# A two-block transformer stage in float32: the rotated partner of each head's features is fetched by transfers between partitions

## Chip, cores and metric

One Trainium2 chip, one core of it. The metric is the device time of one launch in microseconds (us), as a median of several runs; lower is better. Inputs and outputs are float32, and the products are made from pairs of rounded parts (hi and lo), three products for each.

## The reference

Two blocks of two layers each run on 512 tokens of 1024 features. Only the first block's heads matter here. In each of its two layers the normed input is projected to queries, keys and values of three kinds of heads (differential, retention, grouped-query), and the queries and keys get a rotary embedding:

```python
def apply_rope(x, cos_sin):
    cos, sin = cos_sin
    n = x.shape[-1] // 2
    ...
    x1, x2 = x[..., :n], x[..., n:]
    return jnp.concatenate([x1 * c - x2 * s, x2 * c + x1 * s], axis=-1)
...
        dq = partial_rope(rms_norm(dq.reshape(B, S, DIFF_HEADS, 2, DIFF_HEAD_DIM), diff_q_norm[l]))
        rq = apply_rope(rq.reshape(B, S, RET_HEADS, RET_KEY_DIM), rope_ret).astype(f32)
        gq = axial_rope(rms_norm(gq.reshape(B, S, GQA_KV_HEADS, GQA_GROUP, GQA_HEAD_DIM), gqa_q_norm[l]))
```

Differential heads rotate the first 16 of 64 features (two heads' maps side by side: tables at features 0 and 64, half width 8). Retention heads rotate all 128 (half width 64). Grouped-query heads rotate in four groups of 32 (half width 16). Each rope is x times a cosine table plus the partner feature, with a sign, times a sine table.

## The kernel before, in words

**Layout.** Features lie on the 128 partitions and the 512 tokens along the free axis, so the partner of a feature lies on another partition. A weight chunk is 128 columns of a weight matrix over 1024 rows, 512 KB.

**A chunk.** SyncE (SP) loads a chunk into one of four slots of `wraw` (`RAW = 4`): `slot(chunk)` waits until chunk - 4 is done on TensorE (`chunk_done`), so each load goes out when a chunk ends. ScalarE rounds it to `whi` (`weight_hi`, L1702), VectorE makes `wlo` (`weight_lo`, L2300), and TensorE (PE) runs 24 matmuls over it (`chunk_product`, L1053 to L1055), in four parts of six.

**The order.** `head_schedule` writes each layer's heads as a list of steps with due times; the unit is one part, and a chunk is four (`PARTS`). All engines walk the same list in the order of the due times, each taking the steps that are its own, so a step that waits holds back everything behind it on its engine. A layer has 34 such chunks; 21 of them are queries or keys with a rope: 5 of grouped-query heads (chunks 0, 1, 3, 4, 5), 8 of differential heads (every third chunk is a value), 8 of retention heads (two of four). Below, rope 0 to rope 20 are these 21 of the first layer in their order; the second layer repeats them. Chunks 0 and 1 end almost together, the others follow four units apart.

**A rope** with a norm, counted from the end of its projection: ScalarE squares and copies the bank to `rawb` (L1897, L1899); PE sums the squares (`head_norm`, L1196, end + 1.5); ScalarE makes the inverse root (L1734, L1737, end + 1.9); VectorE scales `rawb` (`head_scale`, L2432, end + 2.4) and raises `qn_ready`; PE multiplies `rawb` with a signed permutation matrix from `mats` (`rotate`, L1206, end + 3.5) into one of two AUX banks of PSUM; VectorE makes t1 = x cos (L2441), t2 = partner sin (L2443), and adds them (L2452) (`roped`, end + 3.9), and raises `rope_done`. Without a norm (retention) rotate is due at end + 0.5 and roped at end + 0.9.

**Units.** Between the parts stand the attention units, 32 in a layer, one every 2.85 units of due time from 18 on (numbered unit 0 to unit 31 here). One unit is: two scores (PE, L1222), `peak` (VectorE, negated row maxima, L2468, 0.5 after), `softmax` (ScalarE, L1937, 0.9 after), `weigh` (VectorE, reciprocals and scaling, L2485 to L2495, 1.7 after), `turn` (PE, four transposes, L1234, 2.6 after), `turned` (ScalarE), and after four units `attend` (L1250, L1253). `lo` steps (L2300) stand 1.8 after a unit's start, just behind its weigh. Retention scores (L1228), their weighing by `decay` (L2478) and the final norms are placed between. After the heads come 24 gate chunks and 12 branch chunks, then the output product and the MLP.

**SP** walks the same list and issues only the weight chunks; a pair chunk (grouped-query) is two transfers (L955, L958), the second after the first has landed.

Of the kernel before, what the change touches and what calls it, by code (L numbers as in the profile page):

```python
# [11 lines left out]
ALU = mybir.AluOpType  # L12
AX = mybir.AxisListType

P = 128
# [46 lines left out]

class Step:
# [24 lines left out]
def head_schedule(layer, num):  # L88
# [126 lines left out]
def number_steps(order, num, last):  # L215

    for s in order:
# [19 lines left out]
        elif name == "rotate":  # L237
            s.rope.rot_aux, s.rope.rot = num["aux"](), num["rot"]()
        elif name == "roped":
            r = s.rope  # L240
            r.free_after = 0 if r.hd is None else last.get(("scored", r.hd - 2), 0)
# [253 lines left out]
class Plan:  # L495


    def __init__(self):
# [4 lines left out]
            "gqa mean split final gate norm norm_tile mlp_tile residual x_turn").split()}  # L503
# [45 lines left out]
def constants():  # L549
# [8 lines left out]
    def table(blocks):  # L558
        cos, sin = np.ones((P, SEQ)), np.zeros((P, SEQ))
        rot = np.zeros((P, P))  # L560
        for at, ang in blocks:
            n = ang.shape[1]
            for half in range(2):
                cos[at + half * n:at + (half + 1) * n] = np.cos(ang).T
                sin[at + half * n:at + (half + 1) * n] = np.sin(ang).T
            for j in range(n):
                rot[at + n + j, at + j] = -1.0
                rot[at + j, at + n + j] = 1.0
        return cos, sin, rot
# [9 lines left out]
    mats = np.stack([t[2] for t in tables] + [halves, np.ones((P, P))]).astype(f)  # L579
# [20 lines left out]
def build(nc, a, out):  # L600
    plan = Plan()
    ctx = ExitStack()
    with ctx:
# [25 lines left out]
        mats = sb("mats", [P, 5, P], scope=one_scope)  # L629
# [46 lines left out]
        decay = sb("decay", [P, TOEPLITZ], scope=head_scope)  # L676
        head_scope.close()
# [92 lines left out]
        rot_done, rope_done, turn_done, score_done = sem("rot_done"), sem("rope_done"), sem("turn_done"), sem("score_done")  # L770
# [74 lines left out]
        def _(sp):  # L845
# [102 lines left out]
            for s in plan.layers:  # L948
# [10 lines left out]

                for step in s.heads:  # L960
                    if step.name == "part" and step.index == 0:
                        whole = step.head
                        if whole.chunk == RAW:
                            tables()
                        if whole.kind == "pair":

                            w, at = a["w_in"][l].rearrange("(k p) c -> p k c", p=P), whole.columns
                            half_chunk(whole.chunk, lambda x: [
                                x.rearrange("p (k two c) -> p k two c", two=2, c=64)[:, :, i] for i in range(2)],
                                w[:, :, at:at + 64], w[:, :, at + 256:at + 320])  # L970
                        else:
                            column_chunk(whole.chunk, a["w_in"][l], whole.columns)
                    elif step.name == "branch":
                        w = a["w_branch"][l, step.n][:, 2 * P * step.pair:2 * P * (step.pair + 1)]
                        if step.n == 2:

                            w = w.rearrange("(g j p) c -> g p j c", g=2, p=64)
                            half_chunk(step.chunk, lambda x: [
                                x[64 * g:64 * (g + 1)].rearrange("p (k c) -> p k c", c=2 * P) for g in range(2)], w[0], w[1])
                        else:  # L980
                            r = slot(step.chunk)
                            sp.dma_start(wraw[:, r, :].rearrange("p (k c) -> p k c", c=2 * P),
                                         w.rearrange("(k p) c -> p k c", p=P)).then_inc(raw_in[r], 16)
                    elif step.name == "gate":
                        column_chunk(step.chunk, a["w_in"][l], GATES + D * step.n + P * step.d)
                for j in range(KT):
# [50 lines left out]
        def _(pe):  # L1037
# [47 lines left out]
            def first_sum(k):  # L1085
                pe.wait_ge(sq_ready, k + 1)
                pe.matmul(ps[:, AUX, :], mats[:, 4, :], sq[:, k % 2], start=(k == 0), stop=(k == KT - 1)).then_inc(sq_used, 1)
# [14 lines left out]
            def small_products():  # L1102

                pe.wait_ge(small_sums, 1)
                pe.matmul(ps[:, SCORE + 1, 0:4], mats[:, 4, :], small[:, 16:20], start=True, stop=True)\
                    .then_inc(par_turned, 1)

            def norm(n):

                pe.wait_ge(sq_used, n.sq + n.tiles)  # L1110
                bank_wait(pe, aux_free, n.aux)
                pe.matmul(ps[:, AUX + n.aux % 2], mats[:, 4, :], root[:, n.root % 2], start=True, stop=True)\
                    .then_inc(norm_summed, 1)
# [35 lines left out]
            def half_norm(n):  # L1149

                pe.wait_ge(sq_used, n.sq + n.tiles)
                pe.matmul(ps[:, AUX + n.aux % 2, CTX:SEQ], mats[:, 4, :], root[:, n.root % 2, CTX:SEQ], start=True, stop=True)\
# [19 lines left out]
            for s in plan.layers:  # L1172
                if s.layer:
                    first_pair(s.norm1)
                for step in s.heads:
# [16 lines left out]
                    elif step.name == "head_norm":  # L1192
# [3 lines left out]
                        pe.matmul(ps[:, AUX + r.sum_aux % 2], mats[:, 3, :], sq[:, r.sq % 2], start=True, stop=True)\  # L1196
                            .then_inc(sq_used, 1)
                    elif step.name == "rotate":
                        r = step.rope
                        if r.normed:  # L1200
                            pe.wait_ge(qn_ready, r.norm + 1)
                        else:
                            bank_done(pe, bank_evac, r.tile)
                        bank_wait(pe, aux_free, r.rot_aux)
                        src = rawb[:, r.n % 2]
                        pe.matmul(ps[:, AUX + r.rot_aux % 2], mats[:, r.table, :], src, start=True, stop=True)\  # L1206
                            .then_inc(rot_done, 1)
# [48 lines left out]
                    elif step.name == "ret_mean":  # L1256
                        pe.wait_ge(att_free, step.head.att + 1)
                        bank_wait(pe, aux_free, step.aux)
                        pe.matmul(ps[:, AUX + step.aux % 2], mats[:, 4, :], fo[:, :], start=True, stop=True)\
                            .then_inc(mean_done, 1)  # L1260
                    elif step.name == "final":
                        pe.wait_ge(fsq_ready, step.head.final_sq + 1)
                        bank_wait(pe, aux_free, step.aux)
                        pe.matmul(ps[:, AUX + step.aux % 2], mats[:, 4, :], fsq[:, :], start=True, stop=True)\
# [70 lines left out]
                if s is plan.layers[0]:  # L1335
# [24 lines left out]
                    pe.matmul(ps[:, n.tile % 2, 0:CTX], mats[:, 4, :], root[:, n.root % 2, 0:CTX], start=True, stop=True)\  # L1360
# [885 lines left out]
        def _(dve):  # L2246
# [156 lines left out]
            for s in plan.layers:  # L2403
# [17 lines left out]
                for step in s.heads:  # L2421
# [12 lines left out]
                    elif step.name == "roped":  # L2434
# [3 lines left out]
                        else:  # L2438
# [498 lines left out]
```

## Time and profile before

| what | value |
|---|---|
| median of 3 runs (lowest to highest) | 3703.54 us (3703.32 to 3707.24) |
| the profiled execution's own time | 3707.53 us |
| its span, first to last instruction | 3705.7 us |
| mean granted TensorE clock | 0.993 |
| PE busy | 3603.9 us (97%) |
| VectorE busy | 1724.6 us (47%) |
| ScalarE busy | 1387.7 us (37%) |
| bytes moved by transfers | 303.66 MB, mean 82 GB/s |

Busy time of PE counts overlapping matmuls, and the heads of the two layers fill about 41 to 420 us and 1058 to 1440 us of the span. The profiled execution is 4.0 us longer than the median of the runs; differences are made against it and then taken off the median.

### The profile page before, as it was taken

How to read it: one execution, taken by the hardware profiler on the slowest of the kernel's cores; microseconds unless marked ns; L12 is line 12 of the kernel's file. 1: busy time of each engine (PE TensorE's matmuls, PEld its weight loads, DVE VectorE, ACT ScalarE, POOL GpSimd, SP SyncE). 2: the span in 40 equal slices, each digit the busy share in tenths (PEclk: the TensorE clock that was granted, in tenths of full speed). 3: DMA queues.
4: the chain of work that ended last, by engine and by line, in shares of the span. 5: the costliest groups of instructions: out<-in, count | busy, mean ns of one | idle time of the engine just before them, and what ended most of it. 6: DMA issues, size and time to landing. Idle time of an engine off the chain costs nothing.

```text
span 3705.7 us, 47186 instructions
## 1 busy us (share of the span) xinstructions
PE 3603.9 (97%) x18015; PEld 2690.5 (73%) x18015; DVE 1724.6 (47%) x2504; ACT 1387.7 (37%) x2048; POOL 2.4 (0%) x9
## 2 busy tenths in 40 slices
PE   8999999999999999999999899999999999999998
PEld 5555788777775557887777764488888875369997
DVE  5665434333466644343334445543323355544344
ACT  4554323322245543233222334532322334443333
POOL 0000000000000000000000000000000000000000
PEclk9999999999999999999999999999999999999999
DMA  3111233555521112345655210022222221013332
GB/s 112 46 46 46 74 92 106 144 153 153 150 72 46 46 46 74 91 119 149 168 161 147 65 51 1 1 61 64 63 62 62 63 83 51 1 56 93 91 93 78
DMA packets 570896, 303.66 MB, mean 82 GB/s; under 512 B 26033, under 2 KB 564993, under 8 KB 570753
## 3 DMA queue, kind: packets, MB, share of 16 engines
q1 hardware_dynamic: 570096, 301.36, 28.6%
q8 instruction: 98, 1.61, 0.2%
q14 instruction: 46, 0.37, 0.0%
q10 hardware_dynamic: 656, 0.33, 0.0%
HBM read 299.55 MB, written 2.10 MB: 81 GB/s over the span
## 4 chain that ended last, share of the span: by engine, by line
PE 94%; ACT 2%; DVE 2%; issue 1%; DMA 0%; SPq 0%; DVEq 0%; ACTq 0%
PE ps L1053 14%; PE ps L1054 14%; PE ps L1055 14%; PE ps L1372 10%; PE ps L1374 10%; PE ps L1376 10%; PE ps L1570 2%; PE ps L1552 2%; PE ps L1222 2%; PE ps L1253 1%; PE ps L1137 1%; PE ps L1234 1%; PE ps L1506 1%; PE ps L1206 1%; PE ps L1250 1%
## 5 line engine op out<-in xcount | busy, mean ns | idle before, releaser
L1702 ACT ACTIVATE whi<-wraw 128x1024 fp32r<-128x1024 f32 x448 | 470.7, 1052 | 544.7 <-DMA wraw<-in_w_mlp 246.8
L1053 PE MATMUL ps<-uhi,whi 128*128 128x512 f32 (+1 forms) x1456 | 625.5, 430 | 12.3 <-DVE ulo L2317 5.2
L2300 DVE TENSOR_TENSOR wlo<-wraw,whi 128x1024 fp32r<-128x1024 f32 x448 | 546.0, 1220 | 116.0 <-ACT whi L1702 111.2
L1055 PE MATMUL ps<-uhi,wlo 128*128 128x512 f32 (+1 forms) x1456 | 572.2, 393 | 0.0
L1054 PE MATMUL ps<-ulo,whi 128*128 128x512 f32 (+1 forms) x1456 | 572.2, 393 | 0.0
L1053 PEld LDWEIGHTS ps<-uhi,whi 128*128 128x128 f32 x1456 | 274.1, 188 | 136.2 <-issue 71.5
L1054 PEld LDWEIGHTS ps<-ulo,whi 128*128 128x128 f32 x1456 | 274.5, 189 | 77.4 <-issue 22.8
L1055 PEld LDWEIGHTS ps<-uhi,wlo 128*128 128x128 f32 x1456 | 273.7, 188 | 65.1
L1372 PE MATMUL ps<-u2hi,whi 128*128 128x512 f32 (+1 forms) x1216 | 297.2, 321 | 2.9 <-DVE wlo L2300 2.4
L1374 PE MATMUL ps<-u2lo,whi 128*128 128x512 f32 (+1 forms) x1216 | 293.9, 318 | 0.0
L1372 PE MATMUL ps<-yhi,whi 128*128 128x512 f32 (+1 forms) x960 | 293.0, 356 | 0.0
L1376 PE MATMUL ps<-u2hi,wlo 128*128 128x512 f32 (+1 forms) x1216 | 293.0, 318 | 0.0
L1376 PE MATMUL ps<-yhi,wlo 128*128 128x512 f32 (+1 forms) x960 | 292.4, 356 | 0.0
L1374 PE MATMUL ps<-ylo,whi 128*128 128x512 f32 (+1 forms) x960 | 292.3, 356 | 0.0
L1053 PE MATMUL ps<-bhi,whi 128*128 128x512 f32 (+1 forms) x720 | 285.3, 396 | 0.0
L1055 PE MATMUL ps<-bhi,wlo 128*128 128x512 f32 (+1 forms) x720 | 280.7, 390 | 0.0
L1054 PE MATMUL ps<-blo,whi 128*128 128x512 f32 (+1 forms) x720 | 280.7, 390 | 0.0
L1372 PEld LDWEIGHTS ps<-u2hi,whi 128*128 128x128 f32 x1216 | 191.1, 190 | 26.8 <-issue 7.2
L2701 DVE SCALAR_TENSOR_TENSOR hh<-ps,mod,hh 128x512 f32 (+1 forms) x116 | 73.5, 661 | 284.5 <-PE ps L1376 284.5
L1374 PEld LDWEIGHTS ps<-u2lo,whi 128*128 128x128 f32 x1216 | 190.2, 189 | 17.6 <-issue 0.8
L1376 PEld LDWEIGHTS ps<-u2hi,wlo 128*128 128x128 f32 x1216 | 190.5, 190 | 17.0
L1372 PEld LDWEIGHTS ps<-yhi,whi 128*128 128x128 f32 x960 | 159.5, 188 | 27.9 <-DVE ylo L2753 0.6
(315 smaller groups left out, 4655.0 us busy)
## 6 DMA issues: line engine op xcount, KB each, us to landing
wraw<-in_w_in SPq DMA_DIRECT2D x128, 512.0 KB, 3.8
wraw<-in_w_mlp SPq DMA_DIRECT2D x128, 512.0 KB, 3.9
mod_raw<-in_w_mod SPq DMA_DIRECT2D x96, 512.0 KB, 5.3
wraw<-in_w_mlp_in SPq DMA_DIRECT2D x64, 512.0 KB, 4.3
wraw<-in_w_mlp_out SPq DMA_DIRECT2D x64, 512.0 KB, 4.0
wraw<-in_w_branch SPq DMA_DIRECT2D x16, 512.0 KB, 3.4
wraw<-in_w_out SPq DMA_DIRECT2D x16, 512.0 KB, 3.9
wraw<-in_w_o SPq DMA_DIRECT2D x16, 512.0 KB, 3.8
```

Of the source, the lines that this page charges most:

```text
L1053: pe.matmul(bank, whs[:, i], x_hi[:, k], start=(i == 0), stop=False)
L1054: pe.matmul(bank, whs[:, i], x_lo[:, k], start=False, stop=False)
L1055: last = pe.matmul(bank, wls[:, i], x_hi[:, k], start=False, stop=(i == n - 1))
L1222: pe.matmul(ps[:, SCORE + (step.unit + m) % 2], q[rows, P * step.qt:P * (step.qt + 1)], k[rows, :], start=True, stop=True).then_inc(score_ ...
L1372: pe.matmul(out[:, at:at + hi - lo], whs[:, k], x_hi[:, k, lo:hi], start=(k == 0), stop=False)
L1374: pe.matmul(out[:, at:at + hi - lo], whs[:, k], x_lo[:, k, lo:hi], start=False, stop=False)
L1376: last = pe.matmul(out[:, at:at + hi - lo], wls[:, k], x_hi[:, k, lo:hi], start=False, stop=(k == KT - 1))
L1552: last = pe.matmul(bank, k2[0:QK + 1, step.h % 2, at:at + P], q2[0:QK + 1, step.h % 3, 0:SEQ], start=True, stop=True)
L1570: pe.matmul(ps[own, OUT, :], vv[:, k, cols], wTx[:, k, :], start=(k == 0), stop=(k == 5))
L1702: act.activation(whi[:, r], wraw[:, r], ACT.Copy).then_inc(w_hi, 1)
L2300: dve.tensor_tensor(wlo[:, r], wraw[:, r], whi[:, r].bitcast(F32), ALU.subtract).then_inc(w_split, 1)
L2701: last = dve.scalar_tensor_tensor(hj, ring(n)[:, lo:hi].unsqueeze(1), gate, hj, ALU.mult, ALU.add)
```

## The change

The product with the permutation matrix (`rotate`) and its three matrices go. In its place SP copies the partner rows of `rawb` into a new buffer `rotated` [128, 512] in SBUF, with one transfer for each run of neighbouring partitions: `SWAPS` lists four of 8 partitions for a differential head, two of 64 for a retention head, eight of 16 for a grouped-query head. The sign moves into the sine table. `roped` reads `rotated` where it read a PSUM bank, waits for the transfers instead of PE, and is due 1.0 later than before with a norm and 1.2 later without. On SP's queue the transfers of chunk c stand right behind the load of chunk c + 4 and wait there for `qn_ready` (or for the copy of a retention head) and, since there is one buffer, for the rope before. `room` keeps the place of the three matrices in memory; the load of `mats` shrinks from 320 to 128 KB. In one layer that is 5 x 8 + 8 x 4 + 8 x 2 = 88 transfers for 21 products.

```diff
+SWAPS = [[(at + n * (1 - half), at + n * half, n) for at in starts for half in range(2)]
+         for starts, n in (((0, 64), 8), ((0,), 64), ((0, 32, 64, 96), 16))]
...
-        put(at, "rotate", rope=r)
-        put(at + 0.4, "roped", rope=r)
+        put(at + (1.4 if r.gain is not None else 1.6), "roped", rope=r)
...
-                sin[at + half * n:at + (half + 1) * n] = np.sin(ang).T
...
+                sin[at + half * n:at + (half + 1) * n] = (2 * half - 1) * np.sin(ang).T
...
-        mats = sb("mats", [P, 5, P], scope=one_scope)
+        mats = sb("mats", [P, 2, P], scope=one_scope)
+        sb("room", [P, 3 * P], scope=one_scope)
...
+        rotated = sb("rotated", [P, SEQ], scope=head_scope)
...
+                ropes_of = {step.chunk: step.rope for step in s.heads if step.name == "project" and step.rope}
+
+                def rotations(chunk):
+                    if chunk == s.norm1.chunk + 1:
+                        rotation(chunk - 1)
+                    if chunk > s.norm1.chunk and chunk in ropes_of:
+                        rotation(chunk)
+
+                def rotation(chunk):
+                    r = ropes_of[chunk]
+                    if r.normed:
+                        sp.wait_ge(qn_ready, r.norm + 1)
+                    else:
+                        bank_done(sp, bank_evac, r.tile)
+                    if r.rot:
+                        sp.wait_ge(rope_done, r.rot)
+                    for to, start, n in SWAPS[r.table]:
+                        sp.dma_start(rotated[to:to + n, :], rawb[start:start + n, r.n % 2, :]).then_inc(rot_in, 16)
...
                             column_chunk(whole.chunk, a["w_in"][l], whole.columns)
+                        rotations(whole.chunk - RAW)
...
-                    elif step.name == "rotate":
-                        r = step.rope
-                        if r.normed:
-                            pe.wait_ge(qn_ready, r.norm + 1)
-                        else:
-                            bank_done(pe, bank_evac, r.tile)
-                        bank_wait(pe, aux_free, r.rot_aux)
-                        src = rawb[:, r.n % 2]
-                        pe.matmul(ps[:, AUX + r.rot_aux % 2], mats[:, r.table, :], src, start=True, stop=True)\
-                            .then_inc(rot_done, 1)
...
-                        dve.wait_ge(rot_done, r.rot + 1)
-                        dve.tensor_tensor(t2, ps[:, AUX + r.rot_aux % 2], ropes[:, 2 * r.table + 1], ALU.mult)\
-                            .then_inc(aux_free[r.rot_aux % 2], 1)
-                        bank_done(dve, aux_free, r.rot_aux)
+                        dve.wait_ge(rot_in, 16 * r.rot_in)
+                        link(dve.tensor_tensor(t2, rotated[:, :], ropes[:, 2 * r.table + 1], ALU.mult))
```

## Rows read from the trace of the kernel before

**Rows 1.** Page, part 1: busy us, share of the span, instructions.
```profile
PE 3603.9 (97%) x18015; PEld 2690.5 (73%) x18015; DVE 1724.6 (47%) x2504; ACT 1387.7 (37%) x2048; POOL 2.4 (0%) x9
```

**Rows 2.** Windows: start:end, length, each engine's busy us, granted clock, DMA share, GB/s.
```profile
100.00:150.00 50.00, 48.52 (x213) 30.28 (x213) 33.11 (x61) 28.30 (x57) 0.00 (x0) 1.00 0.18 53
...
450.00:550.00 100.00, 100.00 (x430) 80.32 (x429) 38.12 (x42) 27.17 (x34) 0.00 (x0) 1.00 0.31 93
```

**Rows 3.** Source view of L1206, the product that goes: form and what it waited for.
```profile
L1206 PE MATMUL ps<-rawb,mats x84: 590/592/697, 47.5 to 1399.9; 128*128 128x512 f32 x84
...
  DVE rawb L2432: 6.9, 6
```

**Rows 4.** Chain that ended last, 100 to 160 us: start, us it adds.
```profile
134.64 0.86 PE ps L1206 x2
```

**Rows 5.** Waits of PE's weight-load side: total us, times, longest.
```profile
PEld ps L1234 <- DVE probs L2491: 13.5, 14, 1.5
...
PEld ps L1234 <- DVE probs L2495: 10.5, 13, 1.5
```

**Rows 6.** Source views of L2441 and L2443, VectorE's two products of a rope.
```profile
L2441 DVE TENSOR_TENSOR turned<-rawb,ropes x42: 681/684/693, 48.3 to 1400.8; 128x512 f32<-128x512 f32 x42
...
L2443 DVE TENSOR_TENSOR turned<-ps,ropes x42: 691/692/693, 49.0 to 1401.5; 128x512 f32<-128x512 f32 x42
```

**Rows 7.** Source views of L852 and L955: SP's time to issue one transfer, ns.
```profile
L852 SPq DMA_DIRECT2D prow<-in_attn_norm x1: 495/495/495, 1.8 to 1.8; - x1
...
L852 SPq DMA_DIRECT2D prow<-in_c x1: 295/295/295, 6.7 to 6.7; - x1
...
L955 SPq DMA_DIRECT2D wraw<-in_w_branch x8: 607/607/745, 392.5 to 1574.0; - x8
```

**Rows 8.** DMA issues by line: count, KB each, median us from issue to landing.
```profile
wraw<-in_w_in SPq DMA_DIRECT2D x128, 512.0 KB, 3.8
...
wraw<-in_w_in SPq DMA_DIRECT2D x16, 256.0 KB, 3.0
...
halves_mask<-in_halves_mask SPq DMA_DIRECT2D x1, 1.0 KB, 2.7
```

**Rows 9.** Timeline of all engines, 41 to 64 us: start, us, what [idle before].
```profile
46.14 0.75 DVE L2432 SCALAR_TENSOR_TENSOR rawb<-rawb,par,root 128x512 f32<-128x512 f32 x1
...
49.99 7.25 SPq L883 DMA_DIRECT2D wraw<-in_w_in  x2
...
57.84 1.06 ACT L1702 ACTIVATE whi<-wraw 128x1024 fp32r<-128x1024 f32 x1
...
60.53 0.60 ACT L1734 ACTIVATE root<-ps 128x512 f32<-128x512 f32 x1 [1.62 <-PE ps L1196]
...
62.97 1.29 DVE L2468 TENSOR_REDUCE negmax<-ps 128x1 f32<-128x512 f32 x2 [0.40 <-PE ps L1222]
```

**Rows 10.** Timeline of VectorE, 139 to 158 us, units 10 and 11.
```profile
144.53 0.68 DVE L2441 TENSOR_TENSOR turned<-rawb,ropes 128x512 f32<-128x512 f32 x1
...
149.09 1.22 DVE L2300 TENSOR_TENSOR wlo<-wraw,whi 128x1024 fp32r<-128x1024 f32 x1
150.98 1.29 DVE L2468 TENSOR_REDUCE negmax<-ps 128x1 f32<-128x512 f32 x2 [0.67 <-PE ps L1222]
```

**Rows 11.** Timeline of VectorE, 205 to 222 us, rope 12 and unit 19.
```profile
212.50 0.69 DVE L2441 TENSOR_TENSOR turned<-rawb,ropes 128x512 f32<-128x512 f32 x1
...
218.19 0.16 DVE L2485 RECIPROCAL inv<-sums 128x1 f32<-128x1 f32 x1 [0.57 <-ACT probs L1937]
```

**Rows 12.** Timeline of PE's weight-load side, 142 to 222 us: scores and turns.
```profile
142.16 0.30 PEld L1222 LDWEIGHTS ps<-kb,qb 64*128 64x128 f32 x4 [0.17 <-issue]
...
149.23 0.42 PEld L1234 LDWEIGHTS ps<-ident,probs 128*128 128x128 f32 x4 [1.12 <-DVE probs L2491]
...
214.62 0.30 PEld L1222 LDWEIGHTS ps<-kb,qb 64*128 64x128 f32 x4 [0.36 <-issue]
...
220.10 0.42 PEld L1234 LDWEIGHTS ps<-ident,probs 128*128 128x128 f32 x4 [1.36 <-DVE probs L2491]
```

More of the change, by code:

```diff
@@ L559, in table @@
         cos, sin = np.ones((P, SEQ)), np.zeros((P, SEQ))
-        rot = np.zeros((P, P))
         for at, ang in blocks:
@@ L564, in table @@
                 cos[at + half * n:at + (half + 1) * n] = np.cos(ang).T
-                sin[at + half * n:at + (half + 1) * n] = np.sin(ang).T
[L566 to L569, printed above, removed]
+                sin[at + half * n:at + (half + 1) * n] = (2 * half - 1) * np.sin(ang).T
+        return cos, sin
     partial = angles(pos, 16, 500000.0)
@@ L578, in constants @@
     halves = np.kron(np.eye(2), np.ones((64, 64)))
-    mats = np.stack([t[2] for t in tables] + [halves, np.ones((P, P))]).astype(f)
+    mats = np.stack([halves, np.ones((P, P))]).astype(f)
     x = np.arange(TOEPLITZ)[None, :] - (SEQ - P) - np.arange(P)[:, None]
@@ L983, in _ @@
                                          w.rearrange("(k p) c -> p k c", p=P)).then_inc(raw_in[r], 16)
+                        rotations(step.chunk - RAW)
                     elif step.name == "gate":
                         column_chunk(step.chunk, a["w_in"][l], GATES + D * step.n + P * step.d)
+                        rotations(step.chunk - RAW)
                 for j in range(KT):
@@ L1086, in first_sum @@
                 pe.wait_ge(sq_ready, k + 1)
-                pe.matmul(ps[:, AUX, :], mats[:, 4, :], sq[:, k % 2], start=(k == 0), stop=(k == KT - 1)).then_inc(sq_used, 1)
+                pe.matmul(ps[:, AUX, :], mats[:, 1, :], sq[:, k % 2], start=(k == 0), stop=(k == KT - 1)).then_inc(sq_used, 1)
             for k in range(3):
@@ L1104, in small_products @@
                 pe.wait_ge(small_sums, 1)
-                pe.matmul(ps[:, SCORE + 1, 0:4], mats[:, 4, :], small[:, 16:20], start=True, stop=True)\
+                pe.matmul(ps[:, SCORE + 1, 0:4], mats[:, 1, :], small[:, 16:20], start=True, stop=True)\
                     .then_inc(par_turned, 1)
@@ L1111, in norm @@
                 bank_wait(pe, aux_free, n.aux)
-                pe.matmul(ps[:, AUX + n.aux % 2], mats[:, 4, :], root[:, n.root % 2], start=True, stop=True)\
+                pe.matmul(ps[:, AUX + n.aux % 2], mats[:, 1, :], root[:, n.root % 2], start=True, stop=True)\
                     .then_inc(norm_summed, 1)
@@ L1151, in half_norm @@
                 pe.wait_ge(sq_used, n.sq + n.tiles)
-                pe.matmul(ps[:, AUX + n.aux % 2, CTX:SEQ], mats[:, 4, :], root[:, n.root % 2, CTX:SEQ], start=True, stop=True)\
+                pe.matmul(ps[:, AUX + n.aux % 2, CTX:SEQ], mats[:, 1, :], root[:, n.root % 2, CTX:SEQ], start=True, stop=True)\
                     .then_inc(norm_summed, 1)
@@ L1258, in _ @@
                         bank_wait(pe, aux_free, step.aux)
-                        pe.matmul(ps[:, AUX + step.aux % 2], mats[:, 4, :], fo[:, :], start=True, stop=True)\
+                        pe.matmul(ps[:, AUX + step.aux % 2], mats[:, 1, :], fo[:, :], start=True, stop=True)\
                             .then_inc(mean_done, 1)
@@ L1263, in _ @@
                         bank_wait(pe, aux_free, step.aux)
-                        pe.matmul(ps[:, AUX + step.aux % 2], mats[:, 4, :], fsq[:, :], start=True, stop=True)\
+                        pe.matmul(ps[:, AUX + step.aux % 2], mats[:, 1, :], fsq[:, :], start=True, stop=True)\
                             .then_inc(fsq_used, 1)
@@ L1359, in _ @@
                     pe.wait_ge(early_summed, 2)
-                    pe.matmul(ps[:, n.tile % 2, 0:CTX], mats[:, 4, :], root[:, n.root % 2, 0:CTX], start=True, stop=True)\
+                    pe.matmul(ps[:, n.tile % 2, 0:CTX], mats[:, 1, :], root[:, n.root % 2, 0:CTX], start=True, stop=True)\
                         .then_inc(early_normed, 1)
```

10 lines of the change are left out of this document (5 added, 5 removed).

## The prediction

> **What bounds the kernel now.** I read the page first: PE is busy for 97% of the span and VectorE for 47% [rows 1], so a change can pay if it takes work off PE. The windows then say where that holds fully. In the gate stage PE is busy 100 of 100 us; in the heads' stage, where the change acts, 48.5 of 50, and VectorE 33 of 50 [rows 2]. The small rest matters: it is the sign that two things bind the heads by turns. The source view of L1206 shows the work that goes: 84 matmuls, two for each of 42 rotations, and some waiting for `rawb` in front of them [rows 3]. A matmul's own 592 ns is pipelined; what a rotation adds to the end is read from the chain of waits, 0.86 us for the pair [rows 4]. Last, the waits of PE's weight-load side: the turn of a unit waited for `weigh` 14 times for 13.5 us and 13 times for 10.5 us [rows 5]. The reader is to see that in 27 of the 64 units PE stood still until VectorE had finished the unit's softmax. Where that is so, a microsecond less of PE work between score and turn only makes the wait longer.
>
> **What goes.** 42 x 0.86 = 36.1 us of PE work [rows 4], 1.0% of the span. After the heads PE never rests [rows 2], so what is saved there reaches the end. The smaller load of `mats` may bring 0 to 1 us at the start, where the load queues are full; I take 0.5.
>
> **What comes.** VectorE's work stays: the second product reads SBUF instead of PSUM, and the first one, which reads SBUF already, takes 684 ns against 692 [rows 6]. A rope is three such, 2.1 us. New is the time L from `qn_ready` to the landing of the last transfer. The trace has no transfer within SBUF. SP takes 0.295 us to issue 8 rows and 0.495 for 16; the dearest form, to half the partitions, 0.607 [rows 7]. The smallest load landed 2.7 us after its issue, 256 KB in 3.0 [rows 8]. So for the eight transfers of a grouped-query rope L = 7 x 0.36 + 2.7 = 5.2 us (I take an issue between the two rows; bounds 7 x 0.30 + 2.7 = 4.8 and 7 x 0.65 + 2.7 = 7.3), for the four of a differential rope 3 x 0.30 + 2.7 = 3.6, for the two of a retention rope 0.4 + 3.0 = 3.4, but behind the weight chunk that was issued when the projection ended and needs 3.8 [rows 8]: about 4. Landing itself is bounded below by nothing better than these rows; I take it as it stands, and 2 us more as the far end, since a source in SBUF isn't shown.
>
> The Trainium skill (DMA: Bandwidth & Descriptors, Rules for kernel authors) speaks against the change: many transfers under 64 KB pay mostly overhead and should be one large one. These are 16, 32 and 128 KB. The trace agrees in kind, 1 KB in 2.7 us and 256 KB in 3.0 [rows 8]. Its section Anatomy of one DMA gives about 2.0 us of fixed cost, for another queue; by an estimate with that page's figure L would be 4.5 instead of 5.2 and the sum some 2 us better.
>
> **Rope by rope.** I compared for each of the 21 ropes of the first layer the moment `rawb` was ready with the moment VectorE would want the partner in the new order; the second layer's units lie within 0.3 us of the first's. Outside the first three ropes the room is 4.4 to 7 us where VectorE has work behind the rope, so the differential and retention transfers are hidden by units' peaks and weighs; without that cover a rope would hold VectorE for 1 to 3 us. What costs is the new place in VectorE's order.
>
> - *Free*, 0.86 each: ropes 3, 4, 6, 13, 16, 18, 19, 20. There the rotation stood outside a unit's score to turn or beside an attend, with slack at the next turn. 8 x 0.86 = 6.9 us.
> - *Moved from before a peak to between peak and weigh*: ropes 5, 7, 12, 14. Peak comes earlier, but weigh can't start when its second softmax is ready, 3.6 us after the score (214.62 to 218.19 for unit 19), but when peak and rope are through, 1.1 + 1.3 + 2.1 = 4.5 us after it [rows 11, 12]. Unit 19 already had PE waiting 1.36 us, so it loses 1.0, and rope 12's own rotation gave nothing, since PE waited at the next turn as well. Rope 14 loses 1.35 against 0.86, ropes 5 and 7 lose about 0.45 each against 0.86. Sum 0.39 + 0.46 - 0.97 - 0.49 = -0.6.
> - *Moved from before weigh to behind weigh (and lo)*: ropes 8, 9, 11, 15. In unit 10 the turn came 7.1 us after the score, with 1.12 of waiting [rows 12], because the rope (from 144.53) stood before weigh. Without it the turn can come after 5.2 us. But the rope now runs behind lo (149.09, 1.22 us) and into unit 11, whose peak was at 150.98 and would now be wanted at 149.1: it starts about 1.6 late [rows 10], and unit 11 has no slack. Net +0.26. In the same way rope 9 with rope 10 gives -0.34, rope 11 +0.63, rope 15, whose next unit has 3.9 us of slack, +1.4. Sum +1.95.
> - *Rope 17*: its rotation stood just before a turn that waited: +0.14.
> - *The start*, ropes 0, 1, 2. SP gets `qn_ready` at 46.9 (L2432 ends), issues eight until 49.6, and they land at about 52.1. Rope 0 ends at 53.5 instead of 50.5, and only then may SP issue the eight of rope 1, until 56.2; in front of the load of chunk 6, which went out at 49.99 [rows 9]. Rope 1 ends at about 60, just when its score is due. Chunk 6 lands at 60.0 instead of 53.8, and ScalarE, whose queue has its `weight_hi` (L1702, 57.84) before the inverse root of chunk 3 (60.53), is late with that root by a good microsecond; so is everything on VectorE behind it, down to the first peak, which lands back at about its old 62.97 [rows 9]. So of three rotations and 2.6 us only some 0.3 stay in the first layer and nothing in the second.
>
> Sum for a layer: 6.9 - 0.6 + 1.95 + 0.14 + 0.15 = 8.5 us, for two 17.0, with `mats` 17.5. Half of the 36 us of work turns into waits for VectorE. The profiled execution would come from 3707.5 to 3690.0, and the median from 3703.5 to **3686.0 us**.
>
> **The rivals.**
>
> *All of it comes through* (faster, about 3664). If ScalarE and VectorE catch up in the units with attends, PE gets its 36.1 us, and the 2.8 us or so of real waiting before L1206 too: 3703.5 - 39 = 3664. For it speaks that VectorE is idle a third of the time; against it the 27 waits of rows 5.
>
> *The transfers land late* (no change, 3696 to 3708). If each takes 1 to 2 us longer than my L, ropes 2, 3, 6, 10 and 14 hold VectorE for up to 1.1 to 2 us each, and the start, where two batches follow one another, doubles it: 4 + 2 + 1.5 + 1.2 + 1.1 + 1.1 = 11 us a layer at 2 us, so 22, against 17.5 gained: 3708; at 1 us about 3697. The rule above on small transfers would work this way.
>
> *SP's issue is dear* (slower, about 3714). If each of the eight costs 0.65 us, as the dearest row has it, SP needs 5.2 us a batch instead of 2.9. The start then holds rope 1, chunk 6 and ScalarE behind it some 4 to 5 us longer, and ropes 2, 3 and 4 come 2.3 us later each, together 10 to 12 us a layer, and if the landing is a microsecond late too, 14: 28 in all, 3703.5 - 17.5 + 28 = 3714. It decides from 8.8 us a layer on, which is about 0.5 us an issue together with a landing of 4 us. For it speaks the row of 0.607; against it that runs of 8 and 16 rows never took over 0.5.
>
> *That SP's wait stalls the weight stream* in the steady state I leave out of the chances: a chunk ends every 9 us, `qn_ready` comes 4 to 6 us after it, and the issues fit behind.
>
> **How the numbers follow.** My forecast, within 3676 to 3696, has 0.58; all of it 0.12; late transfers 0.17; dear issues 0.13. A measurement of this kernel can tell about 0.2%, 7.4 us, from no change: faster means under 3696.1, slower over 3711. The first two are faster, late transfers nearly all within. That gives 0.70 faster, 0.17 the same, 0.13 slower. For 8 in 10 the range runs from 3670, which leaves out most of the full gain, to 3704, which leaves out the dear issues and the worst of the late ones.
>
> **What would show it.** L1206 is gone; the L1234 waits for L2491 and L2495 grow from 24 to about 40 us. A wait of VectorE for a transfer stands before L2443 for ropes 0 to 2 in both layers, 2 to 3 us each, and hardly elsewhere. The load of chunk 6 goes out near 56 instead of 50. The heads end 8 to 9 us sooner in the first layer. I am wrong if L2443 waits at most ropes, if an issue within SBUF takes over 0.5 us, or if the waits of L1234 don't grow.

## The result, and the profile after

The changed kernel is **slower**: 3718.93 us (median of six runs, 3712.79 to 3727.97) against 3703.43 us of the kernel before on the same chips, a ratio of 1.0047 with a 95% interval of 1.0036 to 1.0058. The forecast was 3686, its range ended at 3704. The profiled execution took 3712.8 us, 6 less than its own median, so the trace shows somewhat less than the loss. Every run below is compared by its normal executions; one of the eleven of e3 took 11189 us at a granted clock of 0.31 and is left out of its median and ratio.

The work did go, as the page's first part of the kernel after says, to be held against [rows 1]:

```profile
PE 3577.0 (96%) x17931; PEld 2682.8 (72%) x17931; DVE 1723.6 (46%) x2504; ACT 1387.8 (37%) x2048; POOL 2.4 (0%) x9
```

PE has 84 matmuls and 27 us of busy time less. Next the source view of L978, the transfers (least, median and longest ns, times of the first and last; below, who waited for them, us and times):

```profile
L978 SPq DMA_DIRECT2D rotated<-rawb x176: 461/591/1542, 46.0 to 1411.9; - x176
...
  DVE turned L2456: 33.8, 12
```

An issue takes 0.59 us and 0.04 to the next one, not the 0.295 of 8 rows or the 0.495 of 16 in [rows 7]. VectorE waits for the transfers at 12 of 42 ropes, 33.8 us in all; 25.7 us of that are ropes 0, 1 and 2 of the two layers (4.40, 4.64, 4.17; 5.15, 4.60, 2.75), the rest ropes 3, 19 and 20. The chain of the critical work, 45 to 75 us (start, us it adds, what), shows them:

```profile
45.95 0.65 SPq L978
...
49.79 0.59 SPq L978
50.42 1.97 DMA rotated<-rawb
...
52.48 0.70 DVE turned L2456
...
53.21 0.70 DVE gk L2463
...
53.99 0.51 SPq L978
...
58.33 0.59 SPq L978
...
58.97 4.17 DMA wraw<-in_w_in
...
63.16 1.06 ACT whi L1715
...
65.46 0.76 DVE rawb L2445
...
66.23 0.51 SPq L978
...
70.58 3.57 DMA rotated<-rawb
```

Read it downwards. Sixteen issues, and a stop between the eighth and the ninth for rope 0 to finish, hold SP from 45.95 to 58.97. The stop is 3.6 us of these 13 (50.42 to 53.99: the landing, the rope, and only one buffer `rotated`); what a second buffer would give back, no run shows. The load of chunk 6 comes behind them; it went out at 49.99 before [rows 9]. The all-engine timeline of the same kernel says what that does (in brackets the idle time before, and what ended it):

```profile
61.88 1.13 PE L1235 MATMUL ps<-gk,gq 64*128 64x512 f32 x4 [2.62 <-DVE gq L2463]
63.16 1.06 ACT L1715 ACTIVATE whi<-wraw 128x1024 fp32r<-128x1024 f32 x1 [7.82 <-DMA wraw<-in_w_in]
...
66.12 1.28 DVE L2479 TENSOR_REDUCE negmax<-ps 128x1 f32<-128x512 f32 x2
...
69.13 0.66 PE L1247 MATMUL ps<-ident,probs 128*128 128x128 f32 x4 [1.57 <-DVE probs L2506]
```

ScalarE stands 7.82 us for chunk 6, its inverse root behind it is late, and the first peak is at 66.12 instead of 62.97 [rows 9]. The turns (L1247, once L1234) wait longer, from the view of waits of PE's weight-load side (total us, times, longest), for [rows 5]:

```profile
PEld ps L1247 <- DVE probs L2502: 31.4, 18, 3.1
...
PEld ps L1247 <- DVE probs L2506: 22.7, 20, 4.5
```

That is 54.1 us where 24.0 stood. And TensorE's clock no longer keeps its higher level in the heads. The windows view, columns as in [rows 2], first of the kernel before and then of the changed one:

```profile
60.00:100.00 40.00, 38.88 (x167) 23.63 (x166) 24.84 (x47) 22.03 (x45) 0.00 (x0) 1.00 0.14 41
150.00:200.00 50.00, 49.01 (x195) 30.31 (x196) 31.23 (x60) 28.46 (x57) 0.00 (x0) 1.00 0.15 43
```

```profile
60.00:100.00 40.00, 31.88 (x119) 20.36 (x120) 22.52 (x41) 19.80 (x39) 0.00 (x0) 0.87 0.31 82
150.00:200.00 50.00, 44.84 (x175) 28.41 (x174) 31.40 (x60) 26.47 (x54) 0.00 (x0) 0.93 0.20 54
```

A mean of 0.87 over 40 us is some 10 us at 1.2 instead of 2.4 GHz, behind the waits above.

**Where the time went, by markers.** I noted the start of every unit's first score in both traces. Minus means earlier than before. "Free" is the kernel of the first experiment, which has the new places but no transfers.

| marker | after, layer 1 / 2 | free, layer 1 / 2 |
|---|---|---|
| unit 0 | +0.1 / +12.0 | -2.6 / -6.5 |
| unit 3 | +7.7 / +17.0 | -4.0 / -7.8 |
| unit 9 | +5.5 / +14.8 | -6.1 / -10.0 |
| unit 16 | +10.1 / +17.8 | -1.2 / -5.4 |
| unit 24 | +14.2 / +19.0 | -0.2 / -1.1 |
| unit 31 | +12.5 / +17.2 | -2.0 / -2.8 |
| end of the heads (first `ghi` of layer 1, last of layer 2) | +10.3 / +13.4 | -4.1 / -6.6 |

Two places lose: the start of each layer, which only the kernel with transfers loses, and units 9 to 24, which both lose. The columns go on from layer 1 to layer 2, so +12.0 at unit 0 of layer 2 is mostly what layer 1 left. Behind the heads the changed kernel makes up 8 us in this execution: its heads end 13.4 us late and the whole 5.3. There TensorE stood at its lower level for 17.1 us, in the profiled execution before for 31.0 (the traces' records of the granted clock, 1450 to 3690 us). That share is not the change's, since over single executions of the runs below it lies anywhere from 17 to 44 us.

### The profile page after: what moved, and what is told of

The parts are those of the page before. It is cut to its first block, busy times and chain, and to the rows that moved or that the text cites. A ratio compares the mean times of both kernels' runs of the same rounds, so it can differ in the third digit from the quotient of the medians.

```text
span 3711.0 us, 47193 instructions
## 1 busy us (share of the span) xinstructions
PE 3577.0 (96%) x17931; PEld 2682.8 (72%) x17931; DVE 1723.6 (46%) x2504; ACT 1387.8 (37%) x2048; POOL 2.4 (0%) x9
## 4 chain that ended last, share of the span: by engine, by line
PE 89%; DVE 4%; ACT 3%; issue 2%; DMA 1%; SPq 1%; DVEq 0%; ACTq 0%
PE ps L1076 13%; PE ps L1077 13%; PE ps L1078 13%; PE ps L1385 10%; PE ps L1387 10%; PE ps L1389 10%; PE ps L1583 2%; PE ps L1565 2%; PE ps L1235 2%; PE ps L1266 1%; PE ps L1160 1%; PE ps L1247 1%; PE ps L1519 1%; PE ps L1263 1%; PE ps L1485 1%
## 5 line engine op out<-in xcount | busy, mean ns | idle before, releaser
L1076 PE MATMUL ps<-uhi,whi 128*128 128x512 f32 (+1 forms) x1456 | 621.0, 427 | 11.5 <-DVE wlo L2313 4.8
L1077 PEld LDWEIGHTS ps<-ulo,whi 128*128 128x128 f32 x1456 | 276.9, 190 | 72.7 <-issue 17.2
```

The source lines that it names most:

```text
L1076: pe.matmul(bank, whs[:, i], x_hi[:, k], start=(i == 0), stop=False)
L1077: pe.matmul(bank, whs[:, i], x_lo[:, k], start=False, stop=False)
```

## The experiments

All ratios are to the kernel before on the same chip, with 95% intervals. "Free" kernels have no transfers: their second product multiplies `rawb` itself, so the rotation is left out of the computation and the partner costs nothing.

| run | transfers | places | median us | ratio |
|---|---|---|---|---|
| changed kernel | 176 | new | 3718.9 | 1.0047 [1.0036, 1.0058] |
| e1 | none | new | 3697.2 | 0.9980 [0.9971, 0.9989] |
| e2 | none | old | 3684.5 | 0.9946 [0.9932, 0.9960] |
| e3 | 42, one a rope | new | 3698.5 | 0.9983 [0.9974, 0.9993] |
| e4 | 96, ropes 5 to 20 | new | 3704.6 | 1.0007 [0.9998, 1.0016] |
| e5 | 176 | old | 3738.8 | 1.0094 [1.0078, 1.0109] |
| e6 | 96, ropes 5 to 20 | old | 3710.1 | 1.0022 [1.0013, 1.0031] |
| e7 | 32, ropes 13 to 20 | old | 3703.5 | 0.9999 [0.9990, 1.0008] |
| e8 | none, PE work kept | new | 3717.7 | 1.0031 [1.0019, 1.0044] |
| e9 | 144, ropes 2 to 20 | new | 3705.9 | 1.0010 [1.0001, 1.0019] |
| e10 | 176, from GpSimd | new | 3713.3 | 1.0033 [1.0021, 1.0045] |
| e11 | 96, from GpSimd | new | 3706.5 | 1.0008 [0.9999, 1.0016] |
| e12 | 28, ropes 13, 15 to 20 | old | 3692.4 | 0.9972 [0.9961, 0.9982] |
| e13 | none | new but 9, 10, 11 | 3689.3 | 0.9955 [0.9941, 0.9969] |
| e14 | none | old but 9, 10, 11 | 3690.4 | 0.9955 [0.9941, 0.9970] |

### e1 and e2: the partner free, in the new and in the old places

```diff
# e1, against the changed kernel
                 def rotation(chunk):
+                    return
...
-                        dve.wait_ge(rot_in, 16 * r.rot_in)
-                        link(dve.tensor_tensor(t2, rotated[:, :], ropes[:, 2 * r.table + 1], ALU.mult))
+                        link(dve.tensor_tensor(t2, src, ropes[:, 2 * r.table + 1], ALU.mult))
# e2: e1, and
-        put(at + (1.4 if r.gain is not None else 1.6), "roped", rope=r)
+        put(at + 0.4, "roped", rope=r)
```

> The changed kernel without its 176 transfers and without the wait for them: VectorE multiplies rawb itself with the sine table, so the ropes are wrong values, and all else, the new places of the ropes in the order too, stays. It is the ceiling of this change. The theory that the transfers (SP's issues at 0.63 us each and what waits for them) turned the gain into a loss expects about 22 us under the kernel before, 3681: my sum rope by rope without the start's loss, 2 x 10.9. The theory that the new places of the ropes in VectorE's order ate the gain expects less than 10 us under it, above 3693. If all of PE's 36 us came through, it would be 3667.

> As e1_free_partner, but roped is due where it was in the kernel before (0.4 after the place of the product). By the ledger of slacks the four ropes moved behind a peak and the four moved behind weigh lose nothing and gain nothing, which makes about 26 us under the kernel before, 3677, some 4 us better than e1. If the new places help on balance, e2 is slower than e1.

3697.2 and 3684.5 us. For e1 I had 3681 by the transfers and over 3693 by the new places, and for e2 3677, 4 us under e1; it is 12.7 under it. So the loss splits into three. Taking 42 products away is worth 19.0 us of the 36.1 us of work; the new places take back 12.7; the transfers as they are cost 21.8 (3718.9 - 3697.2). 19.0 - 12.7 - 21.8 = -15.5, the result. By the intervals of the ratios each of these terms is known to some 4 to 6 us. The eleven executions of e1 spread from 3691 to 3704, and the profiled one, 3692.5, is among its shorter ones.

What the new places do is in VectorE's timelines. Kernel e1, units 10 and 11:

```profile
142.43 0.75 DVE L2502 SCALAR_TENSOR_TENSOR probs<-probs,inv 128x512 f32<-128x512 f32 x1
143.10 1.22 DVE L2314 TENSOR_TENSOR wlo<-wraw,whi 128x1024 fp32r<-128x1024 f32 x1
144.24 0.69 DVE L2455 TENSOR_TENSOR turned<-rawb,ropes 128x512 f32<-128x512 f32 x1
...
146.41 1.29 DVE L2479 TENSOR_REDUCE negmax<-ps 128x1 f32<-128x512 f32 x2
```

and PE's weight-load side there, from the timeline of that engine:

```profile
143.24 0.42 PEld L1248 LDWEIGHTS ps<-ident,probs 128*128 128x128 f32 x4 [1.79 <-DVE probs L2502]
...
150.46 0.42 PEld L1248 LDWEIGHTS ps<-ident,probs 128*128 128x128 f32 x4 [2.56 <-DVE probs L2502]
152.83 0.51 PEld L1236 LDWEIGHTS ps<-kb,qb 64*128 64x128 f32 x4 [0.65 <-issue]
```

The same unit in e2, where the rope stands before the weigh (first VectorE's peak, then PE's weight-load side):

```profile
145.27 1.29 DVE L2479 TENSOR_REDUCE negmax<-ps 128x1 f32<-128x512 f32 x2 [0.67 <-PE ps L1236]
...
149.62 0.42 PEld L1248 LDWEIGHTS ps<-ident,probs 128*128 128x128 f32 x4 [1.43 <-DVE probs L2502]
151.62 0.30 PEld L1236 LDWEIGHTS ps<-kb,qb 64*128 64x128 f32 x4 [0.37 <-issue]
```

The rope behind the weigh starts at 144.24 and pushes the next unit's peak to 146.41 (145.27 in e2, with PE at the same place within 0.3 us); the next turn waits 2.56 instead of 1.43, and the next score's loads take 0.51 us instead of 0.30: the clock is at its lower level then. In the window from 150 to 200 us e1 was granted 0.93 of the clock, e2 1.00.

### e5: the transfers in the old places

```diff
-        put(at + (1.4 if r.gain is not None else 1.6), "roped", rope=r)
+        put(at + 0.4, "roped", rope=r)
```

> The changed kernel with all its 176 transfers, roped due where it was before. The free-partner pair says that the new places cost 12.7 us when nothing has to be waited for; here VectorE meets the transfers earlier and waits for more of them. If the places cost as much with the transfers, 3706 (15.5 - 12.7 over the kernel before); if the later places are needed to cover the transfers, as they seem meant to, it is no better than the changed kernel, 3719 or more. I expect something between, 3712.

3738.8 us, another 19.9 over the changed kernel and far outside the 3712 that I expected. The source view of its second product says why:

```profile
L2456 DVE TENSOR_TENSOR turned<-rotated,ropes x42: 691/692/694, 53.4 to 1437.6; 128x512 f32<-128x512 f32 x42
...
  DMA rotated<-rawb: 70.9, 26
```

26 ropes wait, 70.9 us. The old places are best for a partner that costs nothing and worst for one that takes 4 to 8 us (the two transfers of a retention rope take 4.1 to 5.1 us from the first issue to the landing of the last in e12, the eight of rope 2 in the changed kernel 7.9). Both the delay and its remedy cost.

### e3: one transfer for a rope

Its 128 rows are copied without the exchange, so the partner is the feature itself, as in the free kernels, but it comes by a transfer.

```diff
-SWAPS = [[(at + n * (1 - half), at + n * half, n) for at in starts for half in range(2)]
-         for starts, n in (((0, 64), 8), ((0,), 64), ((0, 32, 64, 96), 16))]
+SWAPS = [[(0, 0, 128)]] * 3
```

> The changed kernel with one transfer of all 128 rows for each rope in place of eight, four or two; the rows are not swapped, so the ropes are wrong values. Bytes are as many or more, the waits and the places are the same, only the number of issues falls from 176 to 42. The theory that the number of issues costs (0.63 us each in front of the landing and of the next load) expects most of the way back to e1: 10 to 22 us under the kernel before. The theory that landing and its wait cost, whatever the number, expects it within 5 us of the changed kernel, 3714 to 3722.

3698.5 us, 20.4 less than with 176 transfers and 1.3 more than with none. The number that I named, 10 to 22 us under the kernel before, was out of reach, since e1 itself is only 6.3 under it; the way back to e1 came nearly whole. The run also leaves out the exchange of the rows, so it doesn't show whether crossing partitions costs anything by itself. Its source view of the transfers, with the times of landing:

```profile
L977 SPq DMA_DIRECT2D rotated<-rawb x42: 470/471/569, 45.8 to 1390.9; - x42
...
  DVE turned L2455: 6.5, 7
...
DMA to landing us min/median/max: 2.2/2.5/5.0
```

The same 128 rows land 2.5 us after one issue of 0.47. So the bytes and the landing are nearly hidden; the *number* of issues costs. That speaks against the rival of the late landing too: the last of rope 0's eight landed 1.97 us after its issue ended, under the 2.7 of the forecast. The rule on small transfers that the prediction cites from the Trainium skill (DMA: Bandwidth & Descriptors, Rules for kernel authors) holds here, with 20.4 us beside it, though through the queue's issue time and not through the landing.

### e4, e6 and e9: the product back for some ropes

The product, its matrix and its old place return for the grouped-query ropes 0 to 4 (e4; in e6 all other ropes too have their old places), or for ropes 0 and 1 only (e9). The core of the edit:

```diff
+        if r.table in (2,):                       # e9: r.dst == "gk" or (r.dst == "gq" and r.slot == 0)
+            put(at, "rotate", rope=r)
+            put(at + 0.4, "roped", rope=r)
+        else:
+            put(at + (1.4 if r.gain is not None else 1.6), "roped", rope=r)    # e6: at + 0.4
```

> The five grouped-query ropes of each layer get the product back, in its old place (with a clearing of the buffer of rotated rows, 0.5 us); the sixteen others keep the transfers. The theory that the loss is the start (two batches of eight issues one behind the other, the load of chunk 6 behind them) and the eight-issue ropes expects the loss gone: 8 to 12 us under the kernel before, 3692 to 3695. If the loss is spread over all ropes, it is no better than the kernel before, 3703 to 3712.

> As e4_gq_by_product, with the sixteen transferred ropes of a layer also due where they were before. If the new places cost even here, 3695 (9 us under e4, the share of the sixteen ropes); if the wait for four issues and a landing, 5.1 us, bites in the old places, no better than e4, 3704 or more.

> The changed kernel, but ropes 0 and 1 of each layer get the product back (of an unsigned swap, as the sine table has the sign). In the changed kernel the first four units come 7.6 us late against the kernel before in the first layer and 5.0 us more in the second. If that is the start's two batches in a row with the load of chunk 6 behind them, it goes: 10 to 12 us under the changed kernel, 3707 to 3709. If it is ropes 2 to 4 with their eight issues each, hardly anything: 3715 or more.

e4 gives 14.3 us back and e9 13.1. The number for e4, 3692 to 3695, was wrong, because it took the new places to be nearly free (e1 with ten products of 0.86 us put back would be 3705.8, and 3704.6 is near that); the number for e9 was right. So nearly all that the grouped-query transfers cost is in the two ropes of the start, 32 of the 176. In e9 unit 3 stands at +1.3 us, where the changed kernel had +7.7. e6 is 5.5 us slower than e4, where I had hoped for 9 us less: with transfers of differential heads the new places are still the better ones.

### e10 and e11: the same transfers from GpSimd's queue

```diff
# e10: the calls of rotations() on SP go, and on GpSimd stands
+            for s in plan.layers:
+                for step in s.heads:
+                    if step.name == "project" and step.rope:
...
+                        for to, start, n in SWAPS[r.table]:
+                            pool.dma_start(rotated[to:to + n, :], rawb[start:start + n, r.n % 2, :]).then_inc(rot_in, 16)
```

> The changed kernel with the 176 transfers issued by GpSimd, whose queue is idle in the heads, instead of SP; the weight loads have SP to themselves again. If it is the place in SP's queue in front of the loads that costs, it is 5 to 10 us under the changed kernel, 3709 to 3714; if it is the time from the scaled rows to the landing, it is no better, or worse where GpSimd takes longer than 0.63 us to issue one: 3719 to 3740.

> e4_gq_by_product with its 96 transfers issued by GpSimd. There SP's queue held back nothing that anyone waited for, so with equal issue times it is the same as e4, 3704; GpSimd's time to issue shows as a difference, 1 us of landing for each 0.25 us of issue.

e10: 3713.3 us, 5.6 less than from SP. e11, which is e4 with that queue: 3706.5 against 3704.6, no difference. The source view of e10:

```profile
L1061 POOL DMA_DIRECT2D rotated<-rawb x176: 484/497/749, 47.8 to 1414.3; - x176
...
  DVE turned L2465: 38.5, 14
DMA to landing us min/median/max: 1.7/2.0/4.4
```

The weight loads no longer stand behind the transfers, but VectorE waits 38.5 us instead of 33.8. By the medians, what others lose by standing behind the transfers on SP's queue is about a quarter of their 21.8 us, and the rest is that the ropes' own rows come late. That split is a rough one: the intervals of the two ratios overlap, and GpSimd's issue is also shorter, 0.50 against 0.59 us.

### e8: the work of PE kept

Kernel e1 with a product of constants, which nobody reads, where the rotation stood.

```diff
+        put(at, "rotate", rope=r)
...
+                        pe.matmul(ps[:, AUX + r.rot_aux % 2], mats[:, 0, :], ropes[:, 0], start=True, stop=True)\
+                            .then_inc(aux_free[r.rot_aux % 2], 1)
```

> e1_free_partner with PE's work put back: where the rotation stood, PE multiplies two constant tiles of the same shapes, and nobody waits for it. New places, no transfers, PE's work as in the kernel before. If the new places are bad by themselves, it is slower than the kernel before by about the 12.7 us that they cost in e1 against e2, 3716. If the loss came because with less PE work nothing bridges the time until VectorE is done, and the clock then falls in the gaps, the two cancel: within 5 us of the kernel before, 3699 to 3708, and hardly any half-speed stretch in the heads.

3717.7 us. I had thought that the new places hurt because PE had less work to bridge VectorE's lateness. Then they should have cost little here. They cost 14 us against the kernel before by the medians and 11.5 by the ratio (its interval is 7 to 16), as much as the 12.7 between e2 and e1. The theory falls: the places cost with and without PE's work.

The run says something of the clock too. Its windows view:

```profile
40.00:440.00 400.00, 377.54 (x1503) 239.53 (x1504) 227.15 (x389) 196.79 (x357) 0.00 (x0) 0.99 0.17 50
1050.00:1450.00 400.00, 376.52 (x1543) 239.25 (x1542) 233.93 (x412) 198.58 (x368) 0.00 (x0) 1.00 0.18 50
```

The heads keep their clock nearly as before, and still end 11.0 us later. By the records of the granted clock, TensorE stood at its lower level for 10.2 us of e8's heads and for 3.4 before. At 1.2 instead of 2.4 GHz at most half the work of a stretch is lost, so by that estimate the clock holds at most 3.4 of the 11.0 us. In the same way it holds at most 5.1 of the 13.0 us by which the heads of e1 end behind those of e2 (20.5 us at the lower level against 10.2). The larger part is the order itself. It isn't the same units, though: from unit 9 to 16 e8 loses 1.8 and 1.5 us in the two layers, e1 4.9 and 4.6; from unit 16 to 24 e8 loses 4.2 and 4.4, e1 1.0 and 4.3.

### e13 and e14: which ropes' places

```diff
+        placed.append(r)
+        late = 0.4 if len(placed) - 1 in (9, 10, 11) else 1.4 if r.gain is not None else 1.6
+        put(at + late, "roped", rope=r)          # e14: the list holds the other eighteen
```

> Without transfers (second product on rawb itself), new places for all ropes but 9, 10 and 11 of each layer, which go back to their old ones. Theory: the free-partner kernel lost 4.9 us a layer between units 11 and 16, where these three stand, against the same kernel in old places, so putting them back gives 9 to 10 us: 3687 us, and unit 16 of layer 0 stands about 6 us early against before, as in the old places. Rival: the loss comes from many small delays and moves to the next unit that has no room: 3693 to 3697 us.

> Without transfers, the old places for all ropes but 9, 10 and 11 of each layer, which stand in their new ones. Theory: these three alone lose 9 to 10 of the 12.7 us: 3694 us, with stretches of half granted clock between units 11 and 16 of both layers. Rival: they lose only together with the ropes moved ahead of them (8) or behind them (15): 3685 to 3688 us.

By the medians, putting ropes 9, 10 and 11 back gives 7.9 of the 12.7 us and moving only them costs 6.0; I had 9 to 10 for both. By the ratios it is 9 and 3, and the interval of e14 overlaps that of e2. The markers decide: from unit 9 to 16 e14 loses 2.1 us in either layer (-6.1 to -4.0, -11.0 to -8.9) while e2 gains 0.4, so the three alone cost 2.5 a layer, 5 in all. They carry about half; with ropes moved around them they cost more than alone. The markers of e13 show a part of the rest: from unit 18 to 20 it falls from -4.0 to -0.4 in the first layer and from -9.4 to -6.2 in the second, where rope 12 now stands between peak and weigh (unit 19), while e2 loses 1.3 and 1.4 there.

### e7 and e12: a version that gains

Products for the grouped-query and differential ropes, all in old places; two transfers each for the retention ropes 13 to 20 (e7), and in e12 without rope 14.

```diff
# e12 against e7: the condition for the product
-        if r.table in (0, 2):
+        if (r.table != 1 or (r.dst == "k" and r.hd % 8 == 4)):
```

> Only the eight retention ropes of each layer have transfers, two each, in the old places of the order; the thirteen others keep the product. By the ledger seven of the eight rotations there were free and gain 0.86 us each, 6 us a layer: 12 us under the kernel before, 3691, if the landing behind the weight chunk (about 4 us) is covered. If it isn't, VectorE waits 1 to 3 us at each and the gain is under 4 us.

> Transfers (two of 64 rows each) only for the seven ropes 13 and 15 to 20 of each layer; the start, both halves of the two scores' heads, and rope 14 keep the product, and every rope keeps its old place. Reading of the kernel with all ten retention ropes (ratio 0.9999): its units 0 to 21 of layer 0 stood even with before, unit 22 was 1.1 us early, and unit 24, behind the rope that rope 14's late rows pushed back, 3.2 us late. Theory: the transfers are free where the next use is units away, and only the ropes with no room lose; then this kernel gains about 3.5 us a layer, 3696 us, ratio 0.998. Rival: the time that TensorE gives back is only waited out elsewhere in a span that VectorE and ScalarE set, so nothing is gained: 3703 us, ratio 1.000.

("All ten" in it should read all eight, and the "two scores' heads" are the grouped-query and differential ones.) One rope a layer makes the difference between 3703.5 and 3692.4 us. In e7, from the timeline around it (VectorE, then the turn that follows):

```profile
240.22 0.69 DVE L2486 TENSOR_TENSOR turned<-rotated,ropes 128x512 f32<-128x512 f32 x1 [1.94 <-DMA rotated<-rawb]
...
245.73 0.42 PEld L1271 LDWEIGHTS ps<-ident,probs 128*128 128x128 f32 x4 [3.30 <-DVE probs L2532]
```

and in e12:

```profile
236.84 0.69 DVE L2480 TENSOR_TENSOR turned<-ps,ropes 128x512 f32<-128x512 f32 x1
...
242.34 0.42 PEld L1270 LDWEIGHTS ps<-ident,probs 128*128 128x128 f32 x4 [0.59 <-DVE probs L2531]
```

Rope 14 stands right in front of a peak, and its transfer's 1.94 us became 2.7 more at the turn. In e12 ropes 18, 19 and 20 of each layer wait too, 8.6 us in all, and that costs little: the whole gains 10.5 us. For e7 I had expected 3691, so its rival, the wait that isn't covered, was nearer. In the windows of e12 the heads keep their clock:

```profile
40.00:440.00 400.00, 381.55 (x1544) 245.10 (x1545) 232.02 (x392) 198.53 (x358) 0.00 (x0) 1.00 0.21 58
```

The heads of its first layer end 5.0 us sooner than before and those of the second 10.5. That is the whole of its gain, half as much again as the 3.5 a layer that I had expected.

## Why the prediction was wrong, by its own steps

**The start.** The step that failed first is the issue time in "L = 7 x 0.36 + 2.7". I took a value between the rows of 8 and of 16 partitions [rows 7], though each of the eight transfers has 16 partitions and the row for 16 says 0.495. With that row L would have been 7 x 0.50 + 2.7 = 6.2. Nor does the number of rows set the time within SBUF: the issues took 0.59 us (and 0.04) for 16 rows, and a median of 0.62 in e4, which has only those of 8 and 64 rows. The dearest form, which I kept as a bound (0.607), was the right one. L was 6.4 us for ropes 0 and 1 (45.95 to 52.4) against 5.2, inside its bounds, and 7.9 for rope 2 (66.23 to 74.15), above the 7.3. What multiplied it is the row of two batches: chunk 6 went out at 58.97 and not 56, landed at 63.1 and not 60.0. I had a gain of 1.7 us at unit 3 of the first layer (with rope 3 and `mats`) and some 0.9 from the end of the first layer's heads to unit 3 of the second; measured are a loss of 7.7 and one of 6.7. Together that is 17 us of the error.

**The ropes moved behind the weigh.** The second failed step is their ledger, "ropes 8, 9, 11, 15 ... sum +1.95". For ropes 8 to 11 it gives +0.55 a layer; from unit 9 to 16 the changed kernel lost 4.5 and 3.0 us, the free one 4.9 and 4.6. I priced each late peak by itself and called the clock 1.00, as [rows 2] have it; behind waits of 2 to 3 us at the turns there are stretches at the lower level, which the ledger had no term for. This is 8.6 us. The estimate under e8 makes the order the larger part of what the new places cost and the clock the smaller; for these units alone no run separates the two.

**Ropes 12 to 14.** Forecast was a loss of 0.6 a layer, measured from unit 16 to 24 are 4.2 and 1.2, together 4.1 more. These three make some 30 of the 33 us between 3686.0 and 3718.9; the rest is below what single executions tell. For ropes 12 to 14 the runs show one part: in e13, from unit 18 to 20, where rope 12 now stands between peak and weigh, 3.6 and 3.2 us are lost and in e2 1.3 and 1.4, so about 2 a layer where the ledger had 0.97. The rest of that part stays open.

**What held.** From unit 3 to 9 the changed kernel gained 2.1 us in either layer, and so did the free one: there the transfers are hidden, as the step on differential ropes had it. The free ropes at the layer's end gave their share (14.2 to 10.3 from unit 24 to the end of the first layer's heads). In the free kernel in old places only 19.0 of 36.1 us came through, near the "half of the 36 us" of the text. The turn's waits grew from 24.0 to 54.1, more than the 40 I named. Of the three signs of being wrong one came: an issue over 0.5 us. Of the signs of being right, chunk 6 went out later than named (58.97 for 56), VectorE's waits at the start were longer than the 2 to 3 us named (4.2 to 4.6 in the first layer, 2.8 to 5.2 in the second), and the first layer's heads ended 10.3 us later instead of 8 to 9 sooner.

**The rival.** It is "SP's issue is dear", at 0.13, with 3714 us; it named the mechanism, the place and the point of 0.5 us, and came within 5 us. Its sum is near for terms that were not: it had 28 us for the transfers, where e1 shows 21.8, and 17.5 of gain without them, where e1 shows 6.3. "All of it comes through" is excluded: with no transfer at all 3684.5 was the best.

## What to carry to other kernels

Price a transfer by the time that its queue needs for each issue, times the number of issues behind which somebody waits, before its landing and bytes: eight pieces cost 5.0 us of the queue, one piece of the same rows 0.47. Replace a product by a transfer only where the next use lies units away (seven of 21 ropes here), and try each place by itself, since one rope without room took back what seven gave. Moving a step later in an engine's order to cover a latency is a cost of its own; measure it with the latency set to nothing.

## What was unexpected of the hardware

- An issue within SBUF isn't cheaper for fewer partitions: medians in the changed kernel are 0.63 us for 8, 0.59 for 16 and 0.57 for 64, each with 0.04 behind it, and 0.47 for all 128 (e3). From GpSimd it is 0.50, and such rows land 2.0 us after their issue began, the 128 rows from SP (e3) 2.5.
- In a stage where PE is busy for 90% and more, waits of 2 to 3 us had stretches of its lower clock level behind them. That the waits bring them was seen in the order of the records, and not tried by itself. In the windows of 40 to 440 us the mean was 0.97 for the changed kernel, 1.00 for the one before and for e12.
